# Block-diagonal matrices with written zeros in five levels of a triangular inverse

## Chip, cores and metric

The kernel runs on one core of a Trainium2 chip. The metric is the device time of one execution in microseconds (us), lower is better. Work is spread by hand over five engines, each with its own instruction stream: TensorE (PE, with its weight loads shown as PEld), VectorE (DVE), ScalarE (ACT), GpSimd (POOL) and the DMA queue of SyncE (SP). They meet at semaphores only.

## What is computed

One decoder layer for 512 tokens: an input projection, a mixer with two groups of heads (a gated delta rule in chunks of 64 tokens, and sparse attention with an indexer), an output projection, and an expert-retrieval FFN. The change lies within the delta rule, where each chunk of each head needs the inverse of a unit lower triangular matrix of 64 by 64:

```python
def gated_delta_rule(q, k, v, g, beta):
    ...
    a_mat = jnp.where(strict, jnp.einsum('bhncd,bhnsd->bhncs', k_beta, k) * decay, 0.0)
    eye = jnp.eye(c, dtype=F32)
    t_inv = lax.linalg.triangular_solve(a_mat + eye, jnp.broadcast_to(eye, a_mat.shape),
                                        left_side=True, lower=True, unit_diagonal=True)
    u = jnp.einsum('bhncs,bhnse->bhnce', t_inv, v_beta)
    w = jnp.einsum('bhncs,bhnsd->bhncd', t_inv, k_beta * jnp.exp(g)[..., None])
```

There are 4 heads and 8 chunks, so 32 such matrices, all in float32.

## The kernel before

`mixer_stage` writes the instruction stream of each engine by hand; the order in the source is the order on the engine. A semaphore counts finished steps, and a wait stops everything behind it on its engine.

**Layout.** Two chunks lie above each other: chunk 2b on partitions 0 to 63, chunk 2b+1 on partitions 64 to 127 (`halves`), in four column blocks of 64 (`square`). A head's eight matrices thus fill a tile of 128 by 256. `pair` holds for each head the inverse so far, `ti`, and its transpose `tt`, side by side.

**The levels.** The inverse grows by doubling: level 0 is made directly, and levels 1 to 5 each join blocks to the double size. A level has four steps for each head `h`:

1. VectorE masks the transposed matrix `at` with the level's pattern into `mt` (L832, inside `level_mask`; semaphore `mt`). The mask of level k+1 is issued ahead of level k's updates, behind the wait for `x` that frees the buffer.
2. TensorE multiplies `mt` by `ti`, eight products of 64x64 weights by 64 columns (L1197, semaphore `x`), into bank 0 or 1.
3. ScalarE copies the 128 by 256 result to `xs` (L982, semaphore `xs`).
4. TensorE multiplies into bank 4+h: eight products for the new `ti` (L1205) and eight for the new `tt` (L1207), semaphore `tx`. Level 5 has only the latter. VectorE subtracts the result from `pair` (L844, semaphore `level`), which the next level's step 2 waits for.

A float32 product is recorded as two weight loads and two matmuls, so eight products are 16 instructions. Between the heads of levels 1 and 2 TensorE also makes 16 products of the indexer (`index_dots`, L1159), four behind head 1 and four behind head 3 of each level, which ScalarE rectifies (L937) and VectorE accumulates (L733) at points listed in `LEVEL_SUMS`. `LEVEL_BEST` sets where VectorE searches the index scores for their largest values (`take_best`: MAX8 at L741, MATCH_REPLACE8 at L742), two rounds each behind heads 3 of level 3 and 1 and 3 of levels 4 and 5. The first search waits for `fenced`, a masking of the scores that GpSimd makes once they are summed (L694).

Behind level 5 TensorE makes `u` and `w` from `tt` (L1224, L1226), and then a recurrence over the eight chunks begins, with products at L1242, L1247, L1264 and L1265. `mt` lies in the buffer `mt_u` (named `raw` in the rows), where `u` is put later, and `xs` in `x_w` (named `front`), where `w` is put. `mt_u` is also the source of a small DMA of the position-bias strip (L672, semaphore `strip_out`). In the rows `qy` is `pair`, `hi` is `at`, and `cst` holds the masks.

## Time and profile before

| | before |
|---|---|
| runs | 1770.25, 1776.65, 1777.16 us (median 1776.65) |
| profiled execution, its own time | 1779.48 us |
| its span in the profile | 1777.7 us |
| TensorE's mean granted clock over the span | 0.971 |
| instructions in the profile | 29209 |
| PE busy | 1666.9 us (94%) |
| VectorE busy | 1367.8 us (77%) |
| ScalarE, GpSimd busy | 682.9 us (38%), 551.0 us (31%) |
| the five levels | from 208.1 to 250.2 us of the span |

The span is what the profile draws; the time includes 1.8 us around it. The busy shares are means over stages that differ much, so they say little about a stretch of 42 us; the windows below do.

### The profile page before, as it was taken

Reading aid. Unit: us, or ns where it says so; the run is one execution under the profiler, and the core shown is the slowest. Engines: PE = TensorE matmul, PEld = TensorE weight load, DVE = VectorE, ACT = ScalarE, POOL = GpSimd, SP = SyncE. Lnnn points to the kernel's source line nnn. Section 1 sums busy time; section 2 is a strip of 40 time slices with the busy share of each in tenths; the row PEclk is TensorE's granted clock in tenths of the full one; section 3 lists DMA queues with packets and bytes.
Section 4 is the critical chain, followed back from the end, with each engine's and each line's share of the span. In section 5 each row is a group of like instructions: output and inputs, shape, how many; then the busy total and the mean of one; then the engine's idle time right before and its main releaser. Section 6 shows DMA issues by size and latency. Waiting matters only on the chain. (4 is left out here: it accounts for less than half of the span.)

```text
span 1777.7 us, 29209 instructions
## 1 busy us (share of the span) xinstructions
PE 1666.9 (94%) x10471; PEld 1518.3 (85%) x10471; DVE 1367.8 (77%) x2505; ACT 682.9 (38%) x1057; POOL 551.0 (31%) x393
## 2 busy tenths in 40 slices
PE   7998888968998999999899999996999999999997
PEld 5876675546777999999899999996999999999996
DVE  6744568776731789999899989945888888888885
ACT  5574223255332343343344444432333333333333
POOL 5000000014511577777623323312333333322220
PEclk9999997879999999999999999998999999999999
DMA  3320010001233478888778888897999999999992
GB/s 132 98 93 34 1 38 1 24 24 48 83 95 130 147 213 281 280 266 275 246 271 322 320 305 306 321 339 263 381 378 372 384 380 371 386 350 336 362 342 100
DMA packets 149145, 404.50 MB, mean 228 GB/s; under 512 B 14100, under 2 KB 71700, under 8 KB 145592
## 3 DMA queue, kind: packets, MB, share of 16 engines
q1 hardware_dynamic: 108728, 243.86, 41.2%
q0 software_dynamic: 36864, 134.23, 20.0%
q10 hardware_dynamic: 3456, 25.17, 3.6%
q8 instruction: 54, 0.88, 0.2%
q14 instruction: 43, 0.35, 0.1%
HBM read 350.77 MB, written 52.44 MB: 227 GB/s over the span
## 5 line engine op out<-in xcount | busy, mean ns | idle before, releaser
L1801 PE MATMUL bank<-hi_parts,rt_u_hi 128*128 128x384 f32 x1024 | 352.2, 344 | 11.7 <-POOL rt_u_lo L1556 10.7
L1966 PE MATMUL bank<-va_w_hi,va_v_hi 128*128 128x384 f32 x1024 | 343.0, 335 | 17.0 <-DVE va_w_lo L1917 17.0
L1803 PE MATMUL bank<-hi_parts,rt_u_lo 128*128 128x384 f32 x1024 | 344.1, 336 | 0.0
L1802 PE MATMUL bank<-lo_parts,rt_u_hi 128*128 128x384 f32 x1024 | 344.0, 336 | 0.0
L1968 PE MATMUL bank<-va_w_hi,va_v_lo 128*128 128x384 f32 x1024 | 342.8, 335 | 0.0
L1967 PE MATMUL bank<-va_w_lo,va_v_hi 128*128 128x384 f32 x1024 | 342.8, 335 | 0.0
L1516 ACT ACTIVATE rt_u_hi<-raw 128x1024 fp32r<-128x1024 f32 x128 | 135.6, 1060 | 370.2 <-PE bank L1803 368.6
L1894 ACT ACTIVATE va_v_hi<-raw 128x1024 fp32r<-128x1024 f32 x128 | 135.8, 1061 | 338.8 <-PE bank L1968 324.0
L2045 POOL DMA_INDIRECT h<-u_rows_dram,own_experts x128 | 170.0, 1328 | 260.9 <-DVE own_waste L1593 248.4
L2051 POOL DMA_INDIRECT qy<-v_dram,own_experts x128 | 130.1, 1016 | 373.5 <-DVE va_own L1944 368.9
L1917 DVE TENSOR_TENSOR va_v_lo<-raw,va_v_hi 128x1024 fp32r<-128x1024 f32 x128 | 156.6, 1223 | 74.8 <-ACT va_v_hi L1894 74.7
L1556 POOL TENSOR_TENSOR rt_u_lo<-raw,rt_u_hi 128x1024 fp32r<-128x1024 f32 x68 | 167.8, 2468 | 138.1 <-ACT rt_u_hi L1516 137.8
L1966 PEld LDWEIGHTS bank<-va_w_hi,va_v_hi 128*128 128x128 f32 x1024 | 192.9, 188 | 17.3 <-DVE va_v_lo L1917 17.3
L1801 PEld LDWEIGHTS bank<-hi_parts,rt_u_hi 128*128 128x128 f32 x1024 | 193.8, 189 | 15.1 <-POOL rt_u_lo L1556 14.2
L1802 PEld LDWEIGHTS bank<-lo_parts,rt_u_hi 128*128 128x128 f32 x1024 | 194.0, 189 | 0.0
L1803 PEld LDWEIGHTS bank<-hi_parts,rt_u_lo 128*128 128x128 f32 x1024 | 193.5, 189 | 0.0
L1967 PEld LDWEIGHTS bank<-va_w_lo,va_v_hi 128*128 128x128 f32 x1024 | 192.9, 188 | 0.0
L1968 PEld LDWEIGHTS bank<-va_w_hi,va_v_lo 128*128 128x128 f32 x1024 | 192.8, 188 | 0.0
L1944 DVE SCALAR_TENSOR_TENSOR va_own<-qy,own_weights,va_own 128x1024 f32<-128x1024 f32 x128 | 163.6, 1278 | 0.0
L1593 DVE SCALAR_TENSOR_TENSOR own_waste<-h,bank 128x1024 bf16<-128x1024 f32 x104 | 126.5, 1216 | 6.8 <-issue 2.0
L1586 DVE TENSOR_TENSOR rt_u_lo<-raw,rt_u_hi 128x1024 fp32r<-128x1024 f32 x60 | 73.3, 1222 | 33.9 <-ACT rt_u_hi L1516 29.0
L1720 DVE TENSOR_TENSOR qy<-qy,rt_piece 128x1024 bf16<-128x1024 bf16 x144 | 91.0, 687 | 5.2 <-DVE qy L1715 0.2
(345 smaller groups left out, 2695.8 us busy)
## 6 DMA issues: line engine op xcount, KB each, us to landing
raw<-u_dram SPq DMA_DIRECT2D x128, 512.0 KB, 4.4
raw<-v_dram SPq DMA_DIRECT2D x128, 512.0 KB, 7.2
active_scratch<-rt_act SPq DMA_DIRECT2D x128, 192.0 KB, 5.3
gates_scratch<-front ACTq DMA_DIRECT2D x12, 1024.0 KB, 7.2
gates_scratch<-back ACTq DMA_DIRECT2D x12, 1024.0 KB, 8.5
front<-gates_scratch SPq DMA_DIRECT2D x8, 1536.0 KB, 12.1
front<-active_scratch SPq DMA_DIRECT2D x64, 192.0 KB, 9.4
back<-active_scratch SPq DMA_DIRECT2D x64, 192.0 KB, 8.1
```

The costliest lines, as they stand in the source:

```text
L1516: a(u_hi[:, j % 2, :], raw[:, j % 4, :], ACT.Copy).then_inc(u_high, 1)
L1556: nc.gpsimd.tensor_tensor(u_lo[:, e % 2, :], raw[:, e % 4, :], u_hi[:, e % 2, :].bitcast(F32), ALU.subtract).then_inc(u_low, 1)
L1801: mm(bank, u_hi[:, j % 2, cols], hi[:, c, 0:TD], start=c == 0, stop=False)
L1802: mm(bank, u_hi[:, j % 2, cols], lo[:, c, 0:TD], start=False, stop=False)
L1803: last = mm(bank, u_lo[:, j % 2, cols], hi[:, c, 0:TD], start=False, stop=c == DC - 1)
L1894: nc.scalar.activation(v_hi[:, par, :], raw[:, j, :], ACT.Copy).then_inc(v_high, 1)
L1917: nc.vector.tensor_tensor(out, a, high.bitcast(F32), ALU.subtract).then_inc(done, 1)
L1944: nc.vector.scalar_tensor_tensor(own[:], ring[:, j, :], w_own[:, bass.ds(e, 1)], own[:], ALU.mult, ALU.add).then_inc(added, 1)
L1966: mm(bank, v_hi[:, j, cols], w_hi[:, j, :], start=start, stop=False)
L1967: mm(bank, v_hi[:, j, cols], w_lo[:, j, :], start=False, stop=False)
L1968: last = mm(bank, v_lo[:, j, cols], w_hi[:, j, :], start=False, stop=stop)
L2045: t.nc.gpsimd.indirect_dma_start(out=u_ring[:, k % RING, :], out_offset=None, in_=u_rows, in_offset=bass.IndirectOffsetOnAxis(ap=eidx[:, k ...
```

## The change

Step 2 and half of step 4 use whole column blocks of 128 as weights. `mt_u` and `x_w` are cleared once (two memsets on GpSimd), and from then on a head's two chunks of a block lie on the diagonal of a 128x128 matrix with zeros beside them (`squares_of`). One product with 128x128 weights then stands for two with 64x64 weights:

- step 2: four products of 128x128 weights by 64 columns in place of eight of 64x64 (L1204 of the changed kernel).
- step 4: the new `tt` takes four such products with `x_w` as weights (L1214). The new `ti`, where `tt` is the weights, stays with eight products of 64x64 (L1212), now all eight ahead of the four.
- step 1 moves from VectorE to GpSimd, in two instructions of 64 partitions for each head and level, since the two halves go to different columns (L703). They wait for `at` or `x` as before. GpSimd's other work in the mixer stands behind all 40.
- step 3 becomes two copies of 64 partitions on ScalarE (L989).

The subtraction, the indexer's products and all that follows are as before.

```diff
--- before.py
+++ after.py
@@ -575,7 +575,7 @@
 
     nc = t.nc
     s = {n: t.sem("gdn_" + n) for n in (
-        "chain", "ab_t", "ab", "exps", "u1", "log",
+        "chain", "cleared", "ab_t", "ab", "exps", "u1", "log",
         "g", "beta", "cums", "g_col", "decays", "beg", "gl", "grow", "exp3", "tiles_t", "kk",
         "taken", "qk", "a", "a_t", "at", "prep", "mt", "x", "xs", "tx", "level", "uw_t", "u", "w", "zero",
         "ws", "vnew", "out", "o_copy", "ds", "state", "osq", "ossq", "olog", "oinv", "delta_mixed",
@@ -625,7 +625,8 @@
 
         pair = sq[:, 0:H]
         ti, tt = pair[:, :, half0], pair[:, :, half1]
-        mt, xs = mt_u[:, :, half0], x_w[:, :, half0]
+
+        squares_of = lambda ap, h, c: blocks(ap[:, h, :])[halves[c], :, halves[c]]
         gl, eg = tmp[:, 0, half0], up_q[:, 0, :]
         dn, dt = up_q[:, 1, half0], up_q[:, 1, half1]
         am = (up_q[:, 3, half0], up_q[:, 3, half1])
@@ -688,6 +689,21 @@
 
             @block.gpsimd
             def _(pool):
+                pool.wait_ge(s["strip_out"], 16)
+                nc.gpsimd.memset(mt_u, 0.0).then_inc(s["cleared"], 1)
+                nc.gpsimd.memset(x_w, 0.0).then_inc(s["cleared"], 1)
+                pool.wait_ge(s["cleared"], 2)
+                for level in range(1, LEVELS):
+                    for h in range(H):
+                        if level == 1:
+                            pool.wait_ge(s["at"], h + 1)
+                        else:
+                            pool.wait_ge(s["x"], H * (level - 2) + h + 1)
+                        for c, rows in enumerate(halves):
+                            last = nc.gpsimd.tensor_tensor(squares_of(mt_u, h, c), blocks(at[:, h, half0])[rows],
+                                                           t.per_block(K_MT + level)[rows], ALU.mult)
+                        last.then_inc(s["mt"], 1)
+                pool.wait_ge(s["mt"], H * (LEVELS - 1))
                 for b in range(1, NB):
                     pool.wait_ge(s["score"], b * IH)
                     own = score[b][:, b * P:(b + 1) * P]
@@ -825,19 +841,7 @@
                 first_level(H - 1)
                 dve.wait_ge(s["prep"], H)
 
-                dve.wait_ge(s["strip_out"], 16)
-                def level_mask(level, h):
-                    if level > 1:
-                        dve.wait_ge(s["x"], H * (level - 2) + h + 1)
-                    tt_(blocks(mt[:, h, :]), blocks(at[:, h, half0]), t.per_block(K_MT + level),
-                        ALU.mult).then_inc(s["mt"], 1)
-
-                for h in range(H):
-                    level_mask(1, h)
                 for level in range(1, LEVELS):
-                    if level + 1 < LEVELS:
-                        for h in range(H):
-                            level_mask(level + 1, h)
                     for h in range(H):
                         dve.wait_ge(s["tx"], H * (level - 1) + h + 1)
                         both = slice(0, T) if level < LEVELS - 1 else half1
@@ -979,7 +983,11 @@
                 for level in range(1, LEVELS):
                     for h in range(H):
                         act.wait_ge(s["x"], H * (level - 1) + h + 1)
-                        a(xs[:, h, :], t.bank[h % 2][:, half0], ACT.Copy).then_inc(s["xs"], 1)
+                        if level == 1 and h == 0:
+                            act.wait_ge(s["cleared"], 2)
+                        for c, rows in enumerate(halves):
+                            ins = a(squares_of(x_w, h, c), blocks(t.bank[h % 2][rows, half0]), ACT.Copy)
+                        ins.then_inc(s["xs"], 1)
                     if level < 3:
                         for q in range(8 * level - 8, 8 * level):
                             rectify(q)
@@ -1192,19 +1200,18 @@
                             pe.wait_ge(s["up_out"], NIDX)
                         if h >= 2:
                             pe.wait_ge(s["xs"], done + h - 1)
-                        for w in square:
-                            for rows in halves:
-                                last = mm(t.bank[h % 2][rows, w], mt[rows, h, w], ti[rows, h, w], start=True, stop=True)
+                        for b, w in enumerate(square):
+                            last = mm(t.bank[h % 2][:, w], mt_u[:, h, b * P:(b + 1) * P], ti[:, h, w], start=True, stop=True)
                         last.then_inc(s["x"], 1)
                     for h in range(H):
                         pe.wait_ge(s["xs"], done + h + 1)
                         new_ti, new_tt = t.bank[4 + h][:, half0], t.bank[4 + h][:, half1]
-                        for w in square:
-                            if level < LEVELS - 1:
-                                for rows in halves:
-                                    mm(new_ti[rows, w], tt[rows, h, w], xs[rows, h, w], start=True, stop=True)
-                            for rows in halves:
-                                last = mm(new_tt[rows, w], xs[rows, h, w], tt[rows, h, w], start=True, stop=True)
+                        if level < LEVELS - 1:
+                            for b, w in enumerate(square):
+                                for c, rows in enumerate(halves):
+                                    mm(new_ti[rows, w], tt[rows, h, w], squares_of(x_w, h, c)[:, b, :], start=True, stop=True)
+                        for b, w in enumerate(square):
+                            last = mm(new_tt[:, w], x_w[:, h, b * P:(b + 1) * P], tt[:, h, w], start=True, stop=True)
                         last.then_inc(s["tx"], 1)
                         if level < 3 and h % 2:
                             first = 8 * level - 8 + 4 * (h // 2)
```

**TensorE, level 3.** First the stream before, from the first step 2 of level 3 (each row with the semaphores that it waits for, and how often it repeats):

```order
L1197 MATMUL bank<-qy,raw 64x64 [waits gdn_xs,gdn_level,gdn_mt]
L1197 MATMUL bank<-qy,raw 64x64 x7
L1205 MATMUL bank<-front,qy 64x64 [waits gdn_xs]
L1205 MATMUL bank<-front,qy 64x64
L1207 MATMUL bank<-qy,front 64x64 x2
L1205 MATMUL bank<-front,qy 64x64 x2
L1207 MATMUL bank<-qy,front 64x64 x2
```

and the same place in the changed kernel:

```order
L1204 MATMUL bank<-qy,raw 128x64 [waits gdn_xs,gdn_level,gdn_mt]
L1204 MATMUL bank<-qy,raw 128x64 x3
L1212 MATMUL bank<-front,qy 64x64 [waits gdn_xs]
L1212 MATMUL bank<-front,qy 64x64 x7
L1214 MATMUL bank<-qy,front 128x64 x4
L1212 MATMUL bank<-front,qy 64x64 [waits gdn_xs]
L1212 MATMUL bank<-front,qy 64x64 x7
L1214 MATMUL bank<-qy,front 128x64 x4
```

The waits are the same. Products that write 128 partitions stand for two, and the stream now goes from 64x64 weights to 128x128 weights and back once for each head.

**GpSimd, the start of the mixer.** Before, the stage begins with the masking of the scores:

```order
L694 ISA [waits dsa_score]
L694 AFFINE_SELECT proj<-proj 128x128
L694 AFFINE_SELECT proj<-proj 128x128 [waits dsa_score] x2
L698 AFFINE_SELECT qy<-qy 128x2048 [waits dsa_bias]
L508 TENSOR_TENSOR lo_parts<-h,hi_parts 128x128 [waits dsa_mixed] x6
```

and in the changed kernel, with the last of the level masks ahead of it:

```order
L703 TENSOR_TENSOR raw<-hi,cst 64x4x64 [waits gdn_x]
L703 TENSOR_TENSOR raw<-hi,cst 64x4x64
L710 ISA [waits dsa_score,gdn_mt]
L710 AFFINE_SELECT proj<-proj 128x128
L710 AFFINE_SELECT proj<-proj 128x128 [waits dsa_score] x2
L714 AFFINE_SELECT qy<-qy 128x2048 [waits dsa_bias]
```

The first masking of scores (L710) now stands behind the masks of level 5, each of which waits for step 2 of level 4.

**VectorE, from head 3 of level 3 to level 4.** Before:

```order
L844 TENSOR_TENSOR qy<-qy,bank 128x512 [waits gdn_tx] x2
L741 MAX gdn_best<-proj 128x8 [waits dsa_fenced]
L742 MATCH_REPLACE proj<-gdn_best,proj 128x256 [waits gdn_chain]
L741 MAX gdn_best<-proj 128x8 [waits gdn_chain]
L742 MATCH_REPLACE proj<-gdn_best,proj 128x256 [waits gdn_chain]
L832 TENSOR_TENSOR raw<-hi,cst 128x256 [waits gdn_x,gdn_chain]
L832 TENSOR_TENSOR raw<-hi,cst 128x256 [waits gdn_x] x3
L844 TENSOR_TENSOR qy<-qy,bank 128x512 [waits gdn_tx] x2
```

and in the changed kernel:

```order
L848 TENSOR_TENSOR qy<-qy,bank 128x512 [waits gdn_tx] x2
L757 MAX gdn_best<-proj 128x8 [waits dsa_fenced]
L758 MATCH_REPLACE proj<-gdn_best,proj 128x256 [waits gdn_chain]
L757 MAX gdn_best<-proj 128x8 [waits gdn_chain]
L758 MATCH_REPLACE proj<-gdn_best,proj 128x256 [waits gdn_chain]
L848 TENSOR_TENSOR qy<-qy,bank 128x512 [waits gdn_tx,gdn_chain]
L848 TENSOR_TENSOR qy<-qy,bank 128x512 [waits gdn_tx]
```

The four masks are gone from VectorE. Its search still stands ahead of level 4's subtractions and still waits for `fenced`.

## Rows read from the trace of the kernel before

**Rows 1.** The page: its first line and its line of busy times.

```profile
span 1777.7 us, 29209 instructions
PE 1666.9 (94%) x10471; PEld 1518.3 (85%) x10471; DVE 1367.8 (77%) x2505; ACT 682.9 (38%) x1057; POOL 551.0 (31%) x393
```

**Rows 2.** Windows by level: length, busy us (count) of PE, PEld, DVE, ACT, POOL; clock.

```profile
208.10:220.37 12.27, 10.77 (x208) 9.04 (x208) 6.84 (x15) 3.68 (x11) 0.00 (x0) 0.86 0.01 3
220.37:230.73 10.36, 9.32 (x209) 7.60 (x209) 7.99 (x17) 4.18 (x13) 0.00 (x0) 1.00 0.01 3
230.73:236.62 5.89, 5.78 (x192) 5.67 (x193) 4.53 (x10) 2.03 (x6) 0.00 (x0) 1.00 0.01 3
236.62:243.45 6.83, 6.04 (x200) 5.90 (x197) 6.48 (x17) 1.54 (x4) 0.29 (x1) 1.00 0.06 8
243.45:250.20 6.75, 4.36 (x138) 4.09 (x135) 6.00 (x18) 1.54 (x4) 0.00 (x0) 1.00 0.60 229
```

**Rows 3.** Timeline of PEld, levels 3 and 4: start us, length us, engine, line, count.

```profile
230.73 1.01 PEld L1197 LDWEIGHTS bank<-qy,raw 64*64 64x64 f32 x32 [0.33 <-issue]
...
232.88 0.23 PEld L1205 LDWEIGHTS bank<-front,qy 64*64 64x64 f32 x4
...
236.62 1.04 PEld L1197 LDWEIGHTS bank<-qy,raw 64*64 64x64 f32 x32
238.56 0.57 PEld L1197 LDWEIGHTS bank<-qy,raw 64*64 64x64 f32 x16 [0.89 <-issue]
```

**Rows 4.** Timeline of PE: eight instructions of 128 by 128 weights, 128 moving columns.

```profile
165.85 1.04 PE L1102 MATMUL bank<-cst,conv 128*128 128x128 f32 x8
```

**Rows 5.** Timeline of PEld, first chunk of the recurrence: array shapes in turn.

```profile
270.62 0.30 PEld L1264 LDWEIGHTS bank<-front,lo 128*128 128x128 f32 x2 [0.55 <-issue]
270.99 0.29 PEld L1265 LDWEIGHTS bank<-lo 64*128 64x128 f32 x2
271.35 0.30 PEld L1264 LDWEIGHTS bank<-front,lo 128*128 128x128 f32 x2
```

**Rows 6.** Timeline of ScalarE: copies out of PSUM, 128 by 256.

```profile
231.46 0.85 ACT L982 ACTIVATE front<-bank 128x256 f32<-128x256 f32 x2 [0.24 <-PE bank L1197]
...
253.25 0.66 ACT L989 ACTIVATE front<-bank 128x256 f32<-128x256 f32 x2 [5.30 <-PE bank L1226]
```

**Rows 7.** GpSimd's groups by shape, 400 to 500 us: busy us, mean ns.

```profile
L523 POOL TENSOR_TENSOR lo_parts<-h,hi_parts 128x512 fp32r<-128x512 f32 x8 | 13.8, 1759 | 9.5 <-ACT hi_parts L430 9.5
...
L508 POOL TENSOR_TENSOR lo_parts<-h,hi_parts 128x128 fp32r<-128x128 f32 x10 | 5.2, 522 | 15.2 <-ACT h L1035 15.2
L504 POOL TENSOR_TENSOR lo_parts<-h,hi_parts 128x512 fp32r<-128x512 f32 x4 | 5.2, 1303 | 0.0
```

**Rows 8.** Timeline of VectorE from the end of level 3.

```profile
237.80 1.28 DVE L844 TENSOR_TENSOR qy<-qy,bank 128x512 f32<-128x512 f32 x2
239.00 0.42 DVE L741 MAX8 gdn_best<-proj 128x8 f32<-128x256 f32 x1
...
240.96 1.43 DVE L832 TENSOR_TENSOR raw<-hi,cst 128x256 f32<-128x256 f32 x4
```

**Rows 9.** Timeline of GpSimd: its first work in the mixer.

```profile
238.13 0.29 POOL L694 TENSOR_SCALAR_AFFINE_SELECT proj<-proj 128x128 f32<-128x128 f32 x1 [195.33 <-DVE proj L733]
```

**Rows 10.** Timeline: the strip's store, and the start of level 1.

```profile
158.64 0.31 SPq L672 DMA_DIRECT2D strip_scratch<-raw  x1
...
208.10 2.20 DVE L832 TENSOR_TENSOR raw<-hi,cst 128x256 f32<-128x256 f32 x6
208.60 1.05 PEld L1197 LDWEIGHTS bank<-qy,raw 64*64 64x64 f32 x32 [2.09 <-DVE qy L793]
```

**Rows 11.** Timeline of PEld around the first index products of level 1.

```profile
214.22 0.30 PEld L1159 LDWEIGHTS bank<-proj 64*128 64x128 f32 x4
...
216.29 0.19 PEld L1205 LDWEIGHTS bank<-front,qy 64*64 64x64 f32 x4 [0.33 <-issue]
```

**Rows 12.** Window at the half clock within level 1.

```profile
209.62:213.02 3.40, 3.36 (x65) 3.21 (x62) 1.52 (x4) 1.26 (x4) 0.00 (x0) 0.50 0.02 5
```

## Prediction

> **What bounds the kernel now.** I started with the page [rows 1]: PE is busy for 94% of 1777.7 us. That mean is set by the long FFN stages. The change lies in the mixer, so I cut the stretch from the first step 2 of level 1 to the end of level 5 into its levels [rows 2]: 12.27, 10.36, 5.89, 6.83 and 6.75 us, 42.1 us together. The reader should see two regimes there. In levels 1 to 3 PE is busy for 88 to 98% of the time, and VectorE, ScalarE and GpSimd have idle time. In levels 4 and 5 PE is busy for 6.04 of 6.83 and 4.36 of 6.75 us, while VectorE is at 6.48 and 6.00: here the searches hold up the subtraction, and PE waits for it.
>
> Level 3 has no indexer products in it and shows the bare price of a level [rows 3]. Step 2 of four heads runs from 230.73 to 232.88, 2.15 us or 0.54 per head. Step 4 runs to 236.62, 3.74 us or 0.935 per head. A head has 32 instructions in step 4, so an instruction with 64x64 weights costs 0.029 us, and 16 of them 0.47 us. The weight loads follow each other without a pause, so PE itself is the limit: a level gets longer by what PE gets to do. ScalarE and GpSimd matter only if they make PE wait.
>
> In level 4 PEld issues the first two heads at 236.62 and the third only at 238.56, after 0.89 us idle [rows 3]. The third head's subtraction is in the pair that starts at 237.80 [rows 8]. The whole of level 4 is 0.94 us longer than level 3, and the bare price of level 5 (2.15 + 1.87) leaves 2.7 us of its 6.75 as waits.
>
> **Step 2 with whole blocks.** It has 8 instructions per head in place of 16. The price of one is the main term. The nearest full-shape row is eight instructions with 128x128 weights and 128 moving columns [rows 4]: 1.04 us, of which the last one's own length is 0.27, so (1.04 - 0.27) / 7 = 0.110 us each. The changed products move 64 columns, which might be cheaper if the moving side were the limit. But [rows 5] has 128x128 weights with 64 columns: two weight loads take 0.30 us, and one is 0.19 long, so the second starts 0.11 after the first. Loading 128 columns of weights sets the pace, and I take 0.110. Eight are 0.88 us, against 0.54 before: 0.34 more per head, 20 heads, **+6.8 us**.
>
> So what halves the instructions does not halve the work: two products of 64x64 on different quarters of the array ran side by side, and were already as one.
>
> **Step 4.** The `ti` part stays at 0.47 us for 16 instructions. The `tt` part becomes 8 instructions of 0.110, 0.88 us, against 0.47: 20 heads by 0.41, **+8.2 us**.
>
> **Changing the shape.** Each head of levels 1 to 4 now goes from 64x64 to 128x128 and back. In [rows 5] the shape changes after every two instructions, and a full turn of four instructions takes 271.35 - 270.62 = 0.73 us. Four at 0.110 are 0.44, so a change costs 0.145. There are 7 new ones in each of levels 1 and 2 (the indexer's products gave a change before too) and 8 in each of 3 and 4, 30 in all: **+4.3 us**. Lower bound: nothing, if going between these two shapes is free.
>
> The Trainium skill, "TensorE: Matmul & The Clock Gate", Part 2, would let both answers stand. Its step on filling the array says a matmul takes as many cycles as it has moving columns, by which a whole block would cost what one pair of 64x64 did, and the first two terms would shrink to almost nothing. Its step on weight loads says that their time goes with the number of weight columns. The trace agrees with the second [rows 5].
>
> **ScalarE's halves.** Two copies of 128 by 256 issued together (L989) take 0.66 us, where a single one (L982, two in 0.85) took 0.85 / 2 = 0.43 [rows 6]. Half the partitions are priced like all of them. PE's third head of step 2 waits for the first head's copy: it is ready at 0.88 + 0.3 + 0.66 = 1.84 us after the level's start, and PE would be there at 1.76. That is 0.1 per level, **+0.5 us**. If the copies overlap less (0.85 for two), ScalarE needs 3.4 us for four heads while PE needs 3.5: 0.3 per level.
>
> **Masks off VectorE.** Six masks take 2.20 us [rows 10], so 20 take some 7.4 us. Little of it was on the path. At the start PE waited for the first mask: step 2 began at 208.60, and the last input of the inverse is ready where VectorE turns to masks, at 208.10: **-0.45 us**. GpSimd has its masks of level 1 made by then: the strip's store goes out at 158.64 [rows 10], and the memsets and three heads' masks follow long before. The fourth head's mask is needed 2.7 us into level 1. In level 4 and 5 the idle of PE (0.94 and 2.7 us) goes, because PE takes longer for itself and VectorE has 1.5 us less in each: **-3.6 us**.
>
> **Masks on GpSimd.** The trace has no mask there. A GpSimd operation on 128 columns takes 0.52 us and one on 512 takes 1.30 [rows 7]; 256 columns lie at 0.78 on the line between them, whatever the partitions. The bounds are 0.52 and 1.30. Two per head make 1.56 and a level 6.25 us. A changed level takes 10 us or more, so the masks themselves are in time. What they do delay is what stands behind all 40: the masking of scores that VectorE's first search waits for. It ran at 238.13, as soon as the scores were summed [rows 9]. Now it needs the level 5 masks, which need step 2 of level 4. Counted from the start of level 4: head 0's product is there at 1.1, the masks end at 7.4, the scores are masked at 7.8. VectorE stands still from 1.0 until then. Its two rounds took 1.96 us, from the first MAX8 at 239.00 to the masks at 240.96 [rows 8], so the subtraction of head 0 in level 4 is ready at 10.4 and head 1's at 11.0; the next search ends at 12.9, and head 2 is ready at 13.6. PE would start level 5 at 10.2 and reach head 2 at 12.0. It starts heads 0, 1, 2, 3 at 10.4, 11.3, 13.6, 14.5, is through step 2 at 15.4 and through step 4 at 18.9, where it would have been at 17.4: **+1.5 us**. With 0.52 per mask the term is nothing, with 1.30 it is about 5.5.
>
> For two engines at once [rows 7] has a hint: the same shape takes 1.76 in one place and 1.30 in another, a factor of 1.35, which would make a mask 1.05 and the term 3.7. The Trainium skill, "SBUF — State Buffer", section "SBUF: two separate sides", states that VectorE operations with two SBUF inputs and GpSimd exclude each other on a shared port pair; no row here shows which pairs of operations did.
>
> **The half clock.** PE ran at half clock for 3.4 us within level 1 [rows 12]. I leave it in its place; nearly the same work falls into it, +0.2.
>
> **The sum.** 6.8 + 8.2 + 4.3 + 0.5 - 0.45 - 3.6 + 1.5 + 0.2 = **+17.5 us**. Walking the levels one by one gives a check: a level without indexer products is 3.6 for step 2, 4 x 1.35 for step 4 and 8 x 0.145, 10.2 us against 5.89. In level 2 the indexer's two stretches take what is left over 2.15 and 3.74, 4.47 us (one runs from just before 214.22 to 216.29 [rows 11]); with them it is 3.6 + 5.4 + 7 x 0.145 + 4.47 = 14.5 against 10.36, level 1 ends 4.0 later, and levels 4 and 5 take 18.9 against 13.58: 4.0 + 4.15 + 4.3 + 5.3 = +17.75. I take the latter. Everything behind (u, w, the recurrence) waits for level 5's last product on PE and keeps its own pace, so it moves as a whole. The profiled execution took 1779.48 us and would take 1797.2; the median of 1776.65 is 2.8 us below it, so the forecast is 1776.65 + 17.75 = **1794.4 us**.
>
> **Rivals.**
> - *A weight load that isn't hidden* (10%). In [rows 5] each shape runs for two instructions only, so they don't show a long series of 128-column loads with 64 moving columns. If load and matmul ran one behind the other, an instruction would cost 0.110 + 0.055, and 320 of them 17.6 us more: about 1812. Against it: [rows 4], where loads hide fully.
> - *A whole block costs one slot of a pair* (6%), 0.0585 us. Then 320 instructions are 18.7 us, where step 2 and the `tt` part took 20.2: -1.5. With shape changes +4.3, copies +0.5, search +1.5, the start -0.45 and some -2 of VectorE's waits it gives 1779, no change that can be told.
> - *Faster: the count of instructions decides* (4%). Before, instructions with 64x64 weights came each 0.029 us. If issuing sets that pace and not the array, a whole-block one costs 0.029 too, and 320 go away. Step 2 is then bound by ScalarE's 4 x 0.66, and levels 1 to 3 get some 2.0 us shorter each; levels 4 and 5 win the 1.5 us of masks that leave VectorE, and the start 0.45: 1767. This decides only where a whole-block instruction costs under 0.046 us and shape changes are free: 320 x 0.046 = 14.7 against 20.2, and 3.4 from VectorE and the start, make the 8.9 us of a gain that can be told. Against it are [rows 4] and [rows 5], both at 0.110.
> - *The late search at its upper bound* (within the forecast's case): +4 more, 1798 to 1799.
>
> **How the numbers follow.** The forecast's case gets 80%; its own range goes from 1788 (shape changes and late search free) to 1801 (masks at 1.30 and slow copies, or another 3.4 us at half clock behind the inverse). The range runs to 1807 towards the unhidden load. A difference under 0.5%, 8.9 us, is about what a measurement of this kernel can't tell from no change. Faster 0.04, same 0.06, slower 0.90.
>
> **What would show it.** In the profile of the changed kernel: L1204 with 128*128 and 64 columns, 16 instructions of two heads over some 1.76 us; L1214 groups of 8 over 0.88; gaps of about 0.1 at each turn to and from L1212; level 3 at 10.2 us; L703 at 0.78 us mean; L710 first at about 7.8 us into level 4, with VectorE idle for some 7 us ahead of its first MAX8; and the start of the u and w products 18 us later than 250.2. It would be wrong if 128x128 loads with 64 columns came faster than every 0.11 us, or if the stage behind had slack that takes up the delay.

## The result, and the profile after

The changed kernel took 1845.55 us (median of four executions, 1845.0 to 1845.89), against 1776.91 us for the kernel before in the same comparison (1770.25 to 1780.33): a ratio of 1.0388, with a 95% interval from 1.0366 to 1.0410. It is 68.6 us slower. The forecast was 1794.4 us, with a range up to 1807: the direction was right, and the loss is nearly four times the forecast.

The page of the changed kernel, its first lines and its line of granted clock:

```profile
span 1843.6 us, 28614 instructions
PE 1736.4 (94%) x10151; PEld 1579.0 (86%) x10151; DVE 1367.7 (74%) x2485; ACT 690.1 (37%) x1077; POOL 586.8 (32%) x435
...
PEclk9999755787999999999999999998999999999999
```

PE is busy for 69.5 us more than in [rows 1] with 320 instructions fewer. The line of 40 slices, 46 us each, shows where: the fifth to the eighth digit, from 184 to 369 us, are 7, 5, 5 and 7 tenths.

The windows of the five levels, and behind them u and w (length; busy us and count of PE, PEld, DVE, ACT, POOL; granted clock). They answer to [rows 2]:

```profile
209.49:234.38 24.89, 23.95 (x144) 20.15 (x144) 4.47 (x8) 5.17 (x15) 5.78 (x8) 0.50 0.01 2
234.38:259.41 25.03, 24.10 (x145) 20.30 (x144) 6.45 (x12) 5.66 (x17) 5.78 (x8) 0.50 0.00 1
259.41:277.98 18.57, 18.57 (x129) 17.62 (x128) 3.91 (x7) 3.52 (x10) 5.78 (x8) 0.50 0.00 1
277.98:296.59 18.61, 18.61 (x130) 17.67 (x129) 6.32 (x16) 3.03 (x8) 6.07 (x9) 0.50 0.23 85
296.59:310.48 13.89, 13.89 (x66) 13.78 (x65) 5.43 (x16) 3.03 (x8) 0.00 (x0) 0.50 0.00 0
310.48:331.00 20.52, 19.92 (x129) 12.68 (x128) 4.79 (x11) 2.53 (x8) 0.00 (x0) 0.50 0.00 1
```

Every level stands at a clock of 0.50, the lower of PE's two levels, 1.2 GHz. Before, only 3.4 us within level 1 did [rows 12]. The levels take 101.0 us where they took 41.6 from the first step 2 on (208.60 to 250.20). PE is busy for all of levels 3 to 5, so nothing waits there that could be taken away: the work is done at half speed. The same is seen in windows that are cut where the clock changes:

```profile
206.30:209.70 3.40, 0.97 (x19) 0.75 (x18) 2.65 (x5) 1.36 (x3) 1.52 (x2) 1.00 0.01 2
209.70:336.00 126.30, 123.10 (x751) 104.57 (x751) 32.00 (x71) 24.79 (x68) 23.40 (x33) 0.50 0.04 13
336.00:342.00 6.00, 5.13 (x33) 3.89 (x31) 5.07 (x12) 1.64 (x4) 0.00 (x0) 1.00 0.01 3
```

The clock falls at 209.7 us, at the same place as before [rows 12], behind 3.4 us in which PE was busy for 0.97. In the kernel before it was back after 3.4 us. Here it stays down for 126.3 us, through the levels and through u and w, which are not changed at all. It is back at 336.0, behind eight matmuls of the indexer (L1167, from 331.7 us on) and within the first products of the recurrence (L1249).

The timeline of PEld in level 3 and the start of level 4 gives the prices of the single terms (they answer to [rows 3]):

```profile
259.41 6.90 PEld L1204 LDWEIGHTS bank<-qy,raw 128*128 128x128 f32 x32 [0.65 <-issue]
266.43 0.93 PEld L1212 LDWEIGHTS bank<-front,qy 64*64 64x64 f32 x16
267.48 1.78 PEld L1214 LDWEIGHTS bank<-qy,front 128*128 128x128 f32 x8
269.38 0.93 PEld L1212 LDWEIGHTS bank<-front,qy 64*64 64x64 f32 x16
...
277.98 6.95 PEld L1204 LDWEIGHTS bank<-qy,raw 128*128 128x128 f32 x32
```

Thirty-two whole-block loads take 6.90 us, 0.216 each, which is twice 0.108. A head of step 4 takes 267.48 - 266.43 = 1.05 and 269.38 - 267.48 = 1.90, 2.95 us together. The 16 instructions with 64x64 weights and the 8 with 128x128, at twice their forecast prices, would be 2 x (0.47 + 0.88) = 2.70. So the instructions have the forecast prices, only twice, because of the clock, and some 0.25 us is left for the two changes of shape (0.29 was forecast for full clock), which did not double.

The timelines of VectorE and GpSimd show the two effects of the moved masks:

```profile
207.61 0.97 DVE L808 TENSOR_TENSOR qy<-hi,cst 128x256 f32<-128x256 f32 x1 [0.43 <-ACT hi L967]
208.61 0.83 DVE L809 TENSOR_TENSOR qy<-cst,qy 128x256 f32<-128x256 f32 x1
...
287.27 0.43 DVE L757 MAX8 gdn_best<-proj 128x8 f32<-128x256 f32 x1 [8.26 <-POOL proj L710]
```

and of GpSimd:

```profile
207.58 1.58 POOL L703 TENSOR_TENSOR raw<-hi,cst 64x256 f32<-64x256 f32 x2 [3.66 <-ACT hi L967]
...
285.20 1.50 POOL L703 TENSOR_TENSOR raw<-hi,cst 64x256 f32<-64x256 f32 x2 [0.20 <-PE bank L1204]
286.94 0.29 POOL L710 TENSOR_SCALAR_AFFINE_SELECT proj<-proj 128x128 f32<-128x128 f32 x1 [0.25 <-POOL raw L703]
```

A mask for half the partitions takes 0.73 us (the mean of 33 in the levels; two together span 1.50), against a forecast of 0.78. Head 3's level 1 masks run from 207.58 on, and meet the last operations of level 0 on VectorE, a multiply and a subtraction (L808 and L809): these take 0.97 and 0.83 us, where the same form took 0.42 before. Together they cost 0.97 + 0.83 - 2 x 0.42 = 0.96 us more, and level 1 starts at 209.49 instead of 208.60. Of this delay 0.41 us was there before: PE's last products ahead of it (L1186, L1178 in the kernel before) began at 206.38 instead of 205.97. PE's idle time ahead of level 1 grew from 1.98 to 2.43 us. The late search is there as well (VectorE idle for 8.26 us ahead of the MAX8 at 287.27), but PE didn't wait for it at half clock.

### The profile page after: what moved, and what is told of

Same layout as the page of the kernel before. It is cut to its first block and busy times, and to the rows that moved or that the text cites. A ratio compares the mean times of both kernels' runs of the same rounds, so it can differ in the third digit from the quotient of the medians.

```text
span 1843.6 us, 28614 instructions
## 1 busy us (share of the span) xinstructions
PE 1736.4 (94%) x10151; PEld 1579.0 (86%) x10151; DVE 1367.7 (74%) x2485; ACT 690.1 (37%) x1077; POOL 586.8 (32%) x435
## 5 line engine op out<-in xcount | busy, mean ns | idle before, releaser
L1973 PEld LDWEIGHTS bank<-va_w_hi,va_v_hi 128*128 128x128 f32 x1024 | 193.1, 189 | 18.9 <-DVE va_v_lo L1924 18.6
```

The costliest lines, as they stand in the source:

```text
L1973: mm(bank, v_hi[:, j, cols], w_hi[:, j, :], start=start, stop=False)
```

## The experiments

The theory after the result: the clock fell behind the lull ahead of level 1, as it did before, and the products with 128x128 weights and 64 moving columns did not bring it up again. The lull, the columns, the zeros and the two kinds of product can be changed one by one. The rivals were that such products pull the clock down by themselves, that the zeros or the whole-array shape do it, and that the masks on GpSimd have a large part in the loss.

**e1: dense products in the lull.** Changed kernel with three products of 512 columns whose result is not used:

```diff
+                for _ in range(3):
+                    mm(t.bank[2][:], ones, qk[:, 0, :], start=True, stop=True)
                 pe.wait_ge(s["prep"], H)
```

> The changed kernel with three products more on TensorE (128x128 weights, 512 columns, result unused) just ahead of level 1, where it was nearly idle before its clock fell at 209.7 us. Theory 'entry': the levels stay at 1.2 GHz because the lull ahead of level 1 put the clock down and products with 128x128 weights and 64 columns do not bring it up again; entered at 2.4 GHz, they keep it. Then the levels run at full clock, level 3 takes about 9.3 us (half of 18.57), and the time is about 1845 - (101 + 20) / 2 = 1785 to 1800. Rival 'pull down': these products put the clock down by themselves within the first level or two; then the time stays within 1835 to 1848 and levels 3 to 5 are at half clock as now.

Measured: 1806.98 us, beside 1779.29 for the kernel before. Windows by level, the last two cut where the clock changed, and then u and w:

```profile
207.80:222.60 14.80, 13.81 (x146) 11.59 (x145) 3.83 (x7) 5.17 (x15) 5.76 (x8) 1.00 0.01 3
...
237.30:247.70 10.40, 10.35 (x129) 9.70 (x129) 4.21 (x9) 3.49 (x10) 5.76 (x8) 1.00 0.01 2
247.70:258.40 10.70, 10.53 (x130) 9.74 (x129) 3.58 (x10) 3.02 (x8) 6.06 (x9) 1.00 0.19 65
258.40:261.50 3.10, 1.97 (x16) 1.86 (x16) 2.96 (x9) 1.51 (x4) 0.00 (x0) 1.00 0.72 288
261.50:272.00 10.50, 10.42 (x50) 10.34 (x50) 5.31 (x16) 1.51 (x4) 0.00 (x0) 0.50 0.00 0
272.00:292.50 20.50, 19.89 (x129) 12.62 (x128) 4.79 (x11) 2.54 (x8) 0.00 (x0) 0.50 0.00 1
```

Levels 1 to 4 run at full clock from end to end, with exactly the changed products. So without a lull these products, together with the 64x64 ones of the `ti` part, don't put down a clock that is up. Level 3 takes 10.40 us; the prediction had 10.2, and 9.3 was expected for this run by halving 18.57, but the changes of shape don't halve. In level 5, behind waits, the clock falls after all, at 261.5, and then stays down through u and w. The time is above the range that was given for it, for that reason.

**e2: 128 moving columns in place of 64.** The same weights, but `ti` and `tt` side by side as the moving operand. The results of the added columns are written to halves of the banks that are unused or overwritten:

```diff
-    last = mm(t.bank[h % 2][:, w], mt_u[:, h, b * P:(b + 1) * P], ti[:, h, w], start=True, stop=True)
+    two = lambda ap: ap.rearrange("p (k n) -> p k n", k=2)[:, :, w]
+    last = mm(two(t.bank[h % 2][:]), mt_u[:, h, b * P:(b + 1) * P], two(pair[:, h, :]), start=True, stop=True)
...
-    last = mm(new_tt[:, w], x_w[:, h, b * P:(b + 1) * P], tt[:, h, w], start=True, stop=True)
+    last = mm(two(t.bank[4 + h][:]), x_w[:, h, b * P:(b + 1) * P], two(pair[:, h, :]), start=True, stop=True)
```

(and the `ti` part behind it, which overwrites its half).

> The changed kernel in which each product with 128x128 weights moves 128 columns in place of 64 (ti and tt side by side; the added results land in unused or later overwritten halves of the banks). A 128-column load sets the pace at 0.108 us per instruction at full clock either way, so the work costs the same. Theory 'columns': the clock stays down because the array has columns moving through it only about half of the time; with 128 columns it goes up within level 1, and the time is 1785 to 1800. Rival 'shape or zeros': the whole-array shape or the zeros in it keep the clock down; then it stays at half through the levels and the time is 1840 to 1850.

Measured: 1796.63 us, 17.3 above the kernel before beside it. Windows of levels 1, 3 and 5:

```profile
209.10:223.90 14.80, 13.82 (x144) 11.43 (x144) 3.81 (x7) 5.16 (x15) 5.77 (x8) 1.00 0.01 3
...
238.70:249.40 10.70, 10.64 (x130) 9.73 (x129) 4.49 (x9) 3.52 (x10) 5.77 (x8) 1.00 0.01 2
...
260.20:268.80 8.60, 7.50 (x64) 7.27 (x64) 7.21 (x21) 3.02 (x8) 0.00 (x0) 1.00 0.25 98
```

The clock is full in all levels, with the same weights, zeros and shape, and with as many instructions (the `tt` part now stands ahead of the `ti` part). But here it had not fallen ahead of level 1 at all, behind the same 2.43 us of idle PE, so the run alone doesn't show that it can be brought up. e5 does.

**e3: all products back at 64x64**, masks on GpSimd and copies in halves kept.

```diff
-    last = mm(t.bank[h % 2][:, w], mt_u[:, h, b * P:(b + 1) * P], ti[:, h, w], start=True, stop=True)
+    for c, rows in enumerate(halves):
+        last = mm(t.bank[h % 2][rows, w], squares_of(mt_u, h, c)[:, b, :], ti[rows, h, w], start=True, stop=True)
```

(and the `tt` part likewise).

> The changed kernel with all products back at 64x64 weights; masks on GpSimd, copies in halves and the memsets stay. Theory 'entry' or 'columns': the clock goes up within level 1 as in the kernel before, and what is left is the price of the moved masks: start of level 1 about 0.9 us later, the late search 1.5 to 4 us, copies 1 us: 1779 to 1784. Rival: the masks on GpSimd are themselves a part of the large loss (level 1 starts late, VectorE slowed), 1790 or more.

Measured: 1783.21 us, 3.9 above the kernel before. Its levels 4 and 5, and the search that VectorE waits with:

```profile
239.20:249.80 10.60, 6.35 (x203) 6.08 (x199) 6.28 (x13) 3.03 (x8) 6.76 (x10) 1.00 0.22 69
249.80:258.00 8.20, 6.34 (x127) 6.22 (x129) 6.93 (x21) 3.03 (x8) 0.00 (x0) 0.59 0.28 109
```

```profile
247.02 0.43 DVE L757 MAX8 gdn_best<-proj 128x8 f32<-128x256 f32 x1 [3.91 <-POOL proj L710]
```

Level 4 takes 10.60 us in place of 6.83, with PE busy for 6.35: here PE is quick enough to wait for the late search. The price of the moved masks is real, but it is no large part of 68.6 us. In this profile level 5 ends at 258.0, 7.8 us later than before [rows 2], with a stretch at half clock in level 5 (0.59 over the level), from which the clock was back at its end with 64x64 products; the total of this one execution shows only half of the 7.8.

**e4: no zeros.** Both memsets write 0.001, so the off-diagonal blocks of the weights are not zero. The two chunks of a block then mix, and the result is no longer their inverse.

```diff
-                nc.gpsimd.memset(mt_u, 0.0).then_inc(s["cleared"], 1)
-                nc.gpsimd.memset(x_w, 0.0).then_inc(s["cleared"], 1)
+                nc.gpsimd.memset(mt_u, 0.001).then_inc(s["cleared"], 1)
+                nc.gpsimd.memset(x_w, 0.001).then_inc(s["cleared"], 1)
```

> The changed kernel with 0.001 in place of 0.0 in the memsets, so that no weight beside the diagonal blocks is zero (the inverse is then a little off). Theory 'columns': nothing changes, 1843 to 1848, half clock through the levels. Rival 'zeros': the zeros keep the activity of the array low; without them the clock goes up within level 1 and the time falls to 1785 to 1800.

Measured: 1842.82 us (one execution), with levels 2 to 5 at a clock of 0.50. So the zeros are not needed for it. The profile shows one thing more. Level 1 begins at 209.35, and the clock falls only 2.5 us later, when PE had been busy with step 2 all the while:

```profile
209.30:211.80 2.50, 2.40 (x20) 2.29 (x20) 0.00 (x0) 1.16 (x4) 1.21 (x2) 1.00 0.00 0
211.80:214.60 2.80, 2.80 (x16) 2.68 (x14) 0.00 (x0) 1.10 (x3) 2.53 (x5) 0.50 0.02 6
```

In e6, which has the same step 2, it also falls 2.5 us into level 1. In e2, with 128 columns, it doesn't fall there, nor in e7, with 64x64 products in step 2. So these products, coming soon behind a lull, may have a part in the fall as well; how large it is, and why the same lull is followed by a fall in some executions and in others not, these runs don't show. All four executions of the changed kernel and this one took 1842 us or more.

**e5: 128 columns, behind a longer lull.** e2 with eight copies on VectorE ahead of level 1, for which PE waits:

```diff
+                for _ in range(8):
+                    link(nc.vector.tensor_copy(tmp[:, 1, :], qk[:, 0, :]))
+                nc.vector.memset(peak[:], 0.0).then_inc(s["lull"], 1)
                 dve.wait_ge(s["prep"], H)
...
                 pe.wait_ge(s["prep"], H)
+                pe.wait_ge(s["lull"], 1)
```

> The kernel of e2 (128 moving columns) with eight copies of 128x512 put on VectorE ahead of level 1, for which TensorE waits: some 5 us of lull, so that its clock surely falls there. Theory 'columns': the clock comes up again within level 1 although every second product has whole-array weights, and the time is that of e2 plus 5 us for the lull plus 2 us at half clock: 1801 to 1806. Rival 'entry alone': whole-array products never bring the clock up, whatever their columns, and e2 stayed up only because it entered level 1 at full clock; then the levels stay at half clock and the time is 1845 to 1855.

Measured: 1799.68 us. Windows from the lull on: the lull, the start of level 1, its rest, level 2.

```profile
206.90:213.10 6.20, 0.07 (x4) 0.00 (x0) 5.37 (x12) 1.36 (x3) 1.53 (x2) 0.71 0.00 1
213.10:216.30 3.20, 3.16 (x15) 3.19 (x16) 0.00 (x0) 0.76 (x2) 0.97 (x2) 0.50 0.00 0
216.30:229.50 13.20, 12.21 (x132) 9.83 (x131) 3.85 (x7) 4.45 (x13) 4.80 (x7) 1.00 0.01 3
229.50:244.30 14.80, 13.81 (x146) 11.43 (x145) 6.31 (x13) 5.64 (x17) 5.77 (x8) 1.00 0.00 1
```

PE is idle for 6.2 us, the clock is at half when level 1 starts, and after 3.2 us of whole-block products with 128 columns it is full and stays so. This is what separates the theories: the changed kernel, whose clock was down 0.2 us after level 1 began, moved 64 columns behind each load, and its clock was back only after 126 us. The shape of the array is the same in both, and the return falls in step 2, so the other order of step 4 has no part in it. The five levels take 61.3 us here (213.1 to 274.4), 39.7 less than in the changed kernel. (The forecast's range for this run began 1.3 us above the measured time.)

**e6 and e7: one step alone in whole blocks.** e6 keeps step 2 and e7 keeps the `tt` part; the other is at 64x64 weights as in e3.

```diff
# e6: step 4 back at 64x64
-    last = mm(new_tt[:, w], x_w[:, h, b * P:(b + 1) * P], tt[:, h, w], start=True, stop=True)
+    for c, rows in enumerate(halves):
+        last = mm(new_tt[rows, w], squares_of(x_w, h, c)[:, b, :], tt[rows, h, w], start=True, stop=True)
# e7: step 2 back at 64x64
-    last = mm(t.bank[h % 2][:, w], mt_u[:, h, b * P:(b + 1) * P], ti[:, h, w], start=True, stop=True)
+    for c, rows in enumerate(halves):
+        last = mm(t.bank[h % 2][rows, w], squares_of(mt_u, h, c)[:, b, :], ti[rows, h, w], start=True, stop=True)
```

> The changed kernel with step 2 in whole blocks and all of step 4 back at 64x64 weights. Theory 'columns': step 4 moves columns all the time for 3.7 us of each level, so the clock comes up at the first step 4; the price is 6.8 us of step 2 beside e3's +3.9: +9 to +13 over the kernel before, 1788 to 1793. Rival 'any whole block keeps it down': half clock through the levels, 1820 or more.

> The changed kernel with step 2 back at 64x64 weights and step 4 as changed. Theory 'columns': step 2 at 64x64 is short (4 us at half clock) and is followed by long stretches of the new step 4, whose columns move only part of the time; whether it comes up in step 2 is open, but if it does, +8.2 for the tt part and +4 for shape changes beside e3's +3.9 give 1792 to 1798; if not, 1825 to 1835. Rival 'any whole block keeps it down': 1825 or more.

Measured: 1782.91 us (e6) and 1802.60 us (e7). Levels 1 and 3 of e6:

```profile
207.50:222.70 15.20, 14.21 (x176) 12.34 (x176) 3.80 (x7) 5.15 (x15) 5.77 (x8) 0.78 0.01 3
...
234.80:242.70 7.90, 7.84 (x162) 7.57 (x161) 3.19 (x6) 3.55 (x10) 5.78 (x8) 1.00 0.01 2
```

and levels 3 and 5 of e7 (level 5 cut at the clock's fall):

```profile
235.00:244.50 9.50, 8.90 (x163) 8.14 (x162) 4.35 (x9) 3.49 (x10) 5.77 (x8) 1.00 0.02 3
...
254.80:258.00 3.20, 1.33 (x34) 1.23 (x35) 3.06 (x9) 1.51 (x4) 0.00 (x0) 1.00 0.66 264
258.00:266.90 8.90, 8.90 (x66) 8.66 (x66) 5.19 (x16) 1.51 (x4) 0.00 (x0) 0.50 0.01 2
```

In e6 the clock fell within step 2 of level 1 and came up while step 4 ran with 64x64 weights (0.78 over the level); then it was full in levels 2 and 3. In levels 4 and 5, behind waits, it fell twice more (0.84 and 0.73 over the levels) and came back each time, once within step 4 and once 2 us into u and w. Its total missed its range on the low side: level 3 has its price (7.90 us, 1.3 over e3's 6.60), but the stages behind ran some 5 us shorter than in e3, within the spread that single executions show. In e7 the clock was full up to level 5 and fell there, as in e1, which put the total above its range. Since it had not fallen ahead of level 1, e7 doesn't answer whether its step 2 would have brought it back.

**e8 and e11: e2 and e1 again**, in three rounds each.

> The kernel of e2 again, in three rounds, to see whether its full clock is kept each time. Theory 'columns': every execution within 1790 to 1800. Rival 'chance': e2 escaped the lull by where its start fell in time, and some executions take 1840 or more.

> The kernel of e1 again in three rounds: the changed products, entered at full clock. Theory 'entry': each execution keeps full clock through levels 1 to 4 and loses it in level 5, 1803 to 1812. Rival 'chance': some executions fall at the start and take about 1845.

Measured: e8 1796.62 us (1794.73 to 1798.84), ratio 1.0103 [1.0082, 1.0124]. e11 1806.89 us (1805.20 to 1809.76), ratio 1.0164 [1.0148, 1.0179]. Neither had an execution near 1840, so the gain over the changed kernel comes each time, and chance is out. For e8 the times alone can't tell whether the clock stayed up ahead of level 1 or fell and came back within a few us, as in e5; in the profiled execution it stayed up. In the profile of e11 it fell in level 5, as in e1.

**e13: why level 5 lost it in e1.** e1 with 128 moving columns in level 5 alone:

```diff
+    if level == LEVELS - 1:
+        last = mm(two(t.bank[h % 2][:]), mt_u[:, h, b * P:(b + 1) * P], two(pair[:, h, :]), start=True, stop=True)
+    else:
         last = mm(t.bank[h % 2][:, w], mt_u[:, h, b * P:(b + 1) * P], ti[:, h, w], start=True, stop=True)
```

(and its `tt` part likewise).

> The kernel of e1 (changed kernel, dense products ahead of level 1) with 128 moving columns in level 5 alone. In e1 the clock fell in level 5, the only level without 64x64 products, where TensorE also waited for VectorE. Theory 'columns': with 128 columns level 5 keeps it, as in e2: u and w run at full clock, 1791 to 1798. Rival 'waits': the waits of level 5's step 2 pulled it down and it falls again, or it falls later in u and w: 1800 to 1809.

Measured: 1796.59 us, ratio 1.0109 [1.0075, 1.0143]. Level 5 in the timeline of PEld, first of e1, then of e13:

```profile
258.42 1.86 PEld L1206 LDWEIGHTS bank<-qy,raw 128*128 128x128 f32 x16 [0.28 <-issue]
261.55 3.49 PEld L1206 LDWEIGHTS bank<-qy,raw 128*128 128x128 f32 x16 [1.26 <-issue]
264.92 6.95 PEld L1216 LDWEIGHTS bank<-qy,front 128*128 128x128 f32 x32
271.98 0.29 PEld L1233 LDWEIGHTS bank<-conv,qy 64*64 64x64 f32 x4
```

```profile
261.80 1.86 PEld L1208 LDWEIGHTS bank<-qy,raw 128*128 128x128 f32 x16 [0.28 <-issue]
264.92 1.86 PEld L1208 LDWEIGHTS bank<-qy,raw 128*128 128x128 f32 x16 [1.26 <-issue]
266.70 3.65 PEld L1222 LDWEIGHTS bank<-qy,front 128*128 128x128 f32 x32
270.47 0.20 PEld L1241 LDWEIGHTS bank<-conv,qy 64*64 64x64 f32 x4
```

Both have the same wait of 1.26 us in the middle of step 2. With 64 columns the loads behind it are at half clock (3.49 for 16), with 128 they are at full (1.86), and so are u and w. So the wait alone doesn't do it: it takes the products with 64 columns around it (two executions of e13, five of e1's kernel).

**e9, e10, e12, e14, e15: is there a version that beats both?** e9 keeps the kernel before with its 64x64 products and whole copies, moves the masks to GpSimd in one instruction of 128 partitions (but for level 1, head 3), and masks the scores for the first search ahead of the level 5 masks. e10 adds two products of 512 columns in the lull. e12 is the kernel before with these two products alone. e14 and e15 are e9 and e10 again.

```diff
+                for level in range(1, LEVELS):
+                    if level == LEVELS - 1:
+                        fence(1)
+                    for h in range(H - 1 if level == 1 else H):
...
+                        nc.gpsimd.tensor_tensor(blocks(mt[:, h, :]), blocks(at[:, h, half0]), t.per_block(K_MT + level),
+                                                ALU.mult).then_inc(s["mt"], 1)
```

> The kernel before (all products with 64x64 weights, whole copies) with its masks on GpSimd in one instruction of 128 partitions each, all but the one of level 1 and head 3, which would meet VectorE's own masks and stays there; GpSimd masks the scores ahead of its level 5 masks. Theory: e3's +4 came from the late search and the slow start, so both go away, and VectorE's waits in levels 4 and 5 shrink by the masks that leave it: 1772 to 1777, 1 to 4 us below the kernel before. Rival: GpSimd's 0.8 us per mask makes TensorE wait for masks in levels 3 to 5, which are only 6 us long: 1779 to 1785.

> The kernel of e9 with two products of 512 columns (result unused) in the lull ahead of level 1. Theory 'entry': the 3.4 us at half clock within level 1 go away, 1 to 2 us less than e9. Rival: the clock falls anyway, or the two products delay level 1: as e9 or up to 1 us more.

> The kernel before with only the two products of 512 columns (result unused) in the lull ahead of level 1. If e10's gain is the clock's, this shows it alone: no half clock within level 1, 1771 to 1775. Rival: e10's gain came from the masks that leave VectorE, with the late search mended; then this is as before, 1775 to 1778.

> The kernel of e9 again, on the same chip as e15. If e10's gain over e9 is a matter of the clock at the entry of level 1, this stays at 1776 to 1781.

> The kernel of e10 again. Theory 'real': 1768 to 1774, 0.2 to 0.5% below the kernel before. Rival 'spread': as the kernel before, 1774 to 1778, since the two products alone (e12) and the masks alone (e9) gave nothing.

| run | median us | ratio to the kernel before, 95% interval |
|---|---|---|
| e9 | 1779.72 | 1.0013 [1.0001, 1.0026] |
| e14 (e9 again) | 1774.11 | 0.9978 [0.9962, 0.9994] |
| e10 | 1770.44 | 0.9962 [0.9949, 0.9975] |
| e15 (e10 again) | 1774.87 | 0.9977 [0.9961, 0.9994] |
| e12 | 1775.40 | 1.0003 [0.9986, 1.0020] |

Windows of the last three levels in e10:

```profile
230.80:236.70 5.90, 5.79 (x193) 5.68 (x194) 2.97 (x6) 2.00 (x6) 2.77 (x4) 1.00 0.01 3
236.70:243.40 6.70, 5.92 (x198) 5.78 (x196) 6.16 (x17) 1.54 (x4) 3.04 (x5) 1.00 0.18 35
243.40:249.40 6.00, 4.28 (x135) 4.01 (x131) 4.98 (x14) 1.54 (x4) 0.00 (x0) 1.00 0.57 228
```

The rival for e9, that PE would wait for GpSimd's masks, is out, though e9's time (1779.72) fell in the range given for that rival: levels 3 and 4 are 5.90 and 6.70 us long, as before, and level 5 is 0.75 shorter. In one instruction of 128 partitions four masks take 2.77 us, against 5.77 for eight of 64. e10's design was below the kernel before in both comparisons, by 0.2 to 0.4%, and below the changed kernel by 70 us or more. But e9 came out on both sides of the kernel before, and beside e14 e15 is not faster (1774.87 against 1774.11), which is what its rival 'spread' had; e14 came 2 us below its own range. In the first comparison e10 was 9 us below e9, where 1 to 2 were expected. The products in the lull alone (e12) gave nothing. Which part brings the gain stays open, and it is smaller than what a difference of two comparisons of one kernel can be (e9 and e14 differ by 0.35%).

## Why the prediction was wrong

**The step that failed** is the one on the half clock: "PE ran at half clock for 3.4 us within level 1 [rows 12]. I leave it in its place; nearly the same work falls into it, +0.2." It was shown to be worth about 50 us. e2 and e8 do the same work at full clock, with as many instructions and 128 moving columns, and take 1796.6 us: 49 us below the changed kernel. Of these 41.3 lie in the levels (101.0 against 59.7 us), and some 9 in u and w with what follows up to the recurrence. I had read the fall of the clock and its return from the trace, and took both as given by the lull. The return, though, was the work of the 64x64 products in level 1, and these were what the change took away. The rivals had no case for it, and the range allowed for only one more stretch of 3.4 us.

**The rest of the sum held, in part by terms that cancel.** With the clock up, these products cost 1.0103 times the kernel before (e8), 18.6 us by medians; the forecast was 17.75. The single levels are some 0.3 us longer than forecast (14.8 against 14.5, 10.7 against 10.2) and the start came later; against that e2 had none of the 3.4 us at half clock that the forecast left in level 1. Term by term:

- A whole-block instruction: 0.110 us forecast [rows 4, 5]; 0.216 at half clock measured, which is twice 0.108. Step 2 and the `tt` part had their price, and the rivals of a hidden slot, an unhidden load and a pace set by the count of instructions are all out.
- Changes of shape: a head of step 4 with them was forecast at 0.47 + 0.88 + 0.29 = 1.64 us. In e1, which has them at full clock, the four of level 3 lie between these two loads (timeline of PEld, the first of step 4 and the first of level 4):

```profile
241.22 0.54 PEld L1214 LDWEIGHTS bank<-front,qy 64*64 64x64 f32 x16
...
247.66 0.53 PEld L1206 LDWEIGHTS bank<-qy,raw 128*128 128x128 f32 x4
```

6.44 / 4 = 1.61 us for one, so a change of shape costs (1.61 - 0.47 - 0.88) / 2 = 0.13.
- Masks on GpSimd: 0.78 forecast, 0.73 measured. In level 4 of e1 the late search began 8.0 us into the level (MAX8 at 255.65), as forecast with 7.8.
- The start of level 1 was mis-signed. Forecast was 0.45 us earlier; PE's idle time ahead of it became 0.45 us longer (2.43 against 1.98), since head 3's masks on GpSimd slowed VectorE's operations from 0.42 to 0.97 and 0.83 us. The other 0.4 us of the later start stood ahead of the lull. I had seen that two operations can slow each other [rows 7], but priced it for GpSimd alone. The Trainium skill, "SBUF — State Buffer", section "SBUF: two separate sides", says that VectorE operations with two SBUF inputs and GpSimd operations exclude each other on a shared port pair. The trace agrees in so far as these VectorE operations took twice as long beside GpSimd's masks; it doesn't show which one waited for which. In e9, where head 3's mask stayed on VectorE, level 1 of the profiled execution begins at 208.1.
- That everything behind "keeps its own pace" was wrong for u and w: the same instructions took 20.5 us instead of 11.8, since they did not bring the clock up either.

The Trainium skill, "TensorE: Matmul & The Clock Gate", Part 1, describes a clock that falls in idle stretches and is released by a busy engine. The profile of the changed kernel agrees with the first half (0.97 us busy in the 3.4 us ahead of the fall), and not with the second as "busy" is read from the profile: PE was busy for 123.1 of 126.3 us at half clock.

**How sure the cause is.** Shown are: the clock (windows), that filling the lull keeps it up through four levels (e1, e11), that whole-block products with 128 columns bring it up in the same place (e5, one execution) and 64x64 products too (the kernel before, e3, e6), that zeros are not needed (e4), and that in level 5 the same waits are followed by a fall with 64 columns and not with 128 (e13). What the chip counts is not shown by these runs, nor is why the clock fell behind the lull in some executions only and, in e4 and e6, 2.5 us after it. Not shown either is why u and w keep a clock that is up (kernel before) and don't bring up one that is down; the runs show both, and in e6 a return 2 us into u and w, behind a step 4 of 64x64 products.

## What to carry to other kernels

Fewer and larger products are no gain where small ones already ran side by side in the array: compare the time of one full-shape instruction with that of a pair of small ones in the trace first. When a clock falls in a lull and returns, ask which instructions bring it back before you replace them, and count everything behind them at both clocks; here 64 columns behind each whole-block load did not bring it back, and 128 did, at 0.3 us a level or less (level 3: 10.70 us in e2, 10.40 in e1).

## What the runs showed of the hardware

- Busy is not enough to get the clock back: 751 matmuls in 126.3 us, with PE busy for 123.1, stayed at 1.2 GHz. With the moving columns of the whole-block products doubled the levels were 41 us shorter (e2, clock up from the start) or 40 (e5, clock down at the start).
- The clock depends on what it was: the changed products held one that was up through four levels (e1, 208 to 258 us) and did not raise one that was down in five (changed kernel, 209.7 to 310.5 us).
- GpSimd's price for a 256-column multiply did not depend on the partitions: a mean of 0.73 us for 64 (changed kernel) and for 128 (e9, e10).
- Beside a GpSimd multiply a VectorE operation on two SBUF operands took about twice as long (0.83 and 0.97 us, where 0.42 is usual).
